# Moving the operands of a depthwise convolution from SBUF into the free columns of their PSUM banks

## What is computed

```python
def causal_depthwise_conv(u, w, b):   # y[t] = sum_k w[k] * u[t - 2 + k] + b, three taps
    ...

h = rms_norm(x, g_pre_ffn[i])
u = causal_depthwise_conv(h @ w_up[i], conv_w[i], conv_b[i])     # 1024 -> 2 * 2816
gate, val = jnp.split(u, 2, axis=-1)
f = (jax.nn.gelu(gate, approximate=True) * val) @ w_down[i]      # 2816 -> 1024
x = x + rms_norm(f, g_post_ffn[i])
...
km = rms_norm_2(km.reshape(b, -1, MEM_HEADS, MEM_HEAD_DIM), mem_qk_norm[1])   # second layer, 4 heads of 128
```

## Time and profile before

| | before |
|---|---|
| median of 3 executions | 882.14 us (881.25 to 884.82) |
| profiled execution | 886.73 us, of which span 885.0 us |
| PE busy | 832.1 us (94%) |
| DVE busy | 660.9 us (75%) |
| ACT busy | 499.7 us (56%) |
| POOL busy | 321.6 us (36%) |
| mean granted TensorE clock | 0.988 |
| L1930, the taps | 66.9 us |
| chain that ended last | PE 57%, DVE 23%, ACT 9%, issue 7%; DVE YC L1930 5% |

### The profile page before, as it was taken

How to read it: one execution, slowest core, us unless ns; L and a number is a source line. 1 busy time by engine, 2 the same in 40 slices (tenths; PEclk the granted TensorE clock), 3 DMA queues, 4 the chain that set the end, 5 groups by cost and what they waited for, 6 DMA issues and landing times.

```text
span 885.0 us, 16964 instructions
## 1 busy us (share of the span) xinstructions
PE 832.1 (94%) x6722; PEld 794.3 (90%) x6722; DVE 660.9 (75%) x981; ACT 499.7 (56%) x914; POOL 321.6 (36%) x148
## 2 busy tenths in 40 slices
PE   4999999999899999998999889988999999999998
PEld 3998889899899999797999779877998899999998
DVE  6695863898889997657899988865756576667774
ACT  6665645844555666866765574457555545444441
POOL 3743222112332333443656453422454233323321
PEclk8999999999999999999999998999999999999999
DMA  5743234344564756461756452322445457666651
GB/s 206 267 161 98 76 91 141 117 144 158 168 213 149 222 160 190 142 190 49 247 168 201 152 171 73 96 96 72 137 153 168 163 152 224 196 190 192 185 173 49
DMA packets 57246, 137.18 MB, mean 155 GB/s; under 512 B 6352, under 2 KB 27088, under 8 KB 57168
## 3 DMA queue, kind: packets, MB, share of 16 engines
q1 hardware_dynamic: 57168, 136.11, 48.4%
HBM read 135.03 MB, written 1.05 MB: 154 GB/s over the span
## 4 chain that ended last, share of the span: by engine, by line
PE 57%; DVE 23%; ACT 9%; issue 7%; DMA 2%; POOL 1%; SPq 0%; DVEq 0%; ACTq 0%
PE PROD L619 11%; PE PROD L620 10%; PE PROD L621 10%; DVE wlo L1622 6%; DVE YC L1930 5%; ACT whi L1109 4%; DVE RS L1630 3%; PE PROD L681 3%; PE OP L821 2%; DMA raw<-stream 2%; PE OP L619 2%; PE TP L621 2%; PE TP L620 2%; PE TP L619 2%; PE OP L621 2%
## 5 line engine op out<-in xcount | busy, mean ns | idle before, releaser
L602 POOL TENSOR_TENSOR wlo<-raw,whi 128x1024 fp32r<-128x1024 f32 x124 | 318.2, 2572 | 542.8 <-ACT whi L1109 518.6
L619 PE MATMUL PROD<-HA,whi 128*128 128x256 f32 x1080 | 306.8, 284 | 14.4 <-DVE HA L1651 6.0
L620 PE MATMUL PROD<-HA,wlo 128*128 128x256 f32 x1080 | 301.8, 279 | 0.0
L621 PE MATMUL PROD<-HA,whi 128*128 128x256 f32 x1080 | 301.7, 279 | 0.0
L1109 ACT ACTIVATE whi<-raw 128x1024 fp32r<-128x1024 f32 x252 | 261.8, 1053 | 39.7 <-PE PROD L621 21.1
L1622 DVE TENSOR_TENSOR wlo<-raw,whi 128x1024 fp32r<-128x1024 f32 x128 | 192.7, 1510 | 77.8 <-ACT whi L1109 77.7
L619 PEld LDWEIGHTS PROD<-HA,whi 128*128 128x128 f32 x1080 | 205.8, 191 | 17.7 <-DVE HA L1651 6.4
L620 PEld LDWEIGHTS PROD<-HA,wlo 128*128 128x128 f32 x1080 | 205.5, 190 | 0.6 <-issue 0.5
L621 PEld LDWEIGHTS PROD<-HA,whi 128*128 128x128 f32 x1080 | 205.1, 190 | 0.0
L1930 DVE SCALAR_TENSOR_TENSOR YC<-Y,CV,YC 128x255 f32<-128x255 f32 x88 | 66.9, 762 | 2.2 <-ACT YC L1333 0.7
L619 PE MATMUL OP<-HA,whi 128*128 128x256 f32 x200 | 57.2, 286 | 1.5 <-DVE wlo L1622 0.8
(11 more groups left out here) (322 smaller groups left out, 1648.4 us busy)
## 6 DMA issues: line engine op xcount, KB each, us to landing
raw<-stream SPq DMA_DIRECT2D x197, 512.0 KB, 4.0
raw<-stream SPq DMA_DIRECT2D x144, 128.0 KB, 2.4
raw<-stream SPq DMA_DIRECT2D x28, 256.0 KB, 2.9
raw<-stream SPq DMA_DIRECT2D x4, 384.0 KB, 3.4
X<-xT SPq DMA_DIRECT2D x2, 512.0 KB, 5.6
out<-X SPq DMA_DIRECT2D x8, 128.0 KB, 2.0
KMEM<-memT SPq DMA_DIRECT2D x1, 512.0 KB, 5.4
VMEM<-memT SPq DMA_DIRECT2D x1, 512.0 KB, 6.1
```

Of the source, the lines that this page charges most:

```text
L602: nc.gpsimd.tensor_tensor(wlo[:, n % NSPLIT, :], raw[:, n % NRAW, :], whi[:, n % NSPLIT, :].bitcast(F32), ALU.subtract).then_inc(lo_pool, 1)
L619: nc.tensor.matmul(dst, wh, hi, start=start, stop=False, skip_group_check=True)
L620: nc.tensor.matmul(dst, wl, hi, start=False, stop=False, skip_group_check=True)
L621: last = nc.tensor.matmul(dst, wh, lo, start=False, stop=stop, skip_group_check=True)
```

## The change

The gate half's scaled product is written into columns 256 to 511 of its own bank and read there by ScalarE and by the taps, whose sum stays in `YC` in SBUF. The up half's scaled product stays in `UU` in SBUF, while its sum of taps, the product with the gelu and the sources of the high and the low part lie in columns 256 to 511 of its bank. So every instruction of VectorE on these halves has one tensor input in SBUF and one in PSUM; the low part (`act_low`) becomes a tensor_tensor. A gate bank is freed by its second tap, no longer by the scaling, and an up bank by the low part of its chunk. The memory statistics leave the rotation for the two banks of `TP`, and the first down pass waits until both their roots are taken. TensorE's matmuls, the stream's tiles, the transfers and the order of work on each engine stay as they were.

```diff
--- before.py
+++ after.py
@@ -204,12 +204,14 @@
 
 
 PLAIN_STATS = ("gk", "gv", "kcT", "vc", "lnmean")
-FFN_OUTS = {(n, m) for n in ("up", "up2") for m in range(2 * FC)} | {("stat", "memk0"), ("stat", "memk1")}
+FFN_OUTS = {(n, m) for n in ("up", "up2") for m in range(2 * FC)}
 BANK, PREV, FREE_COUNT = {}, {}, {}
 _last, _seen, _c = {}, [-NBANK + i for i in range(NBANK)] + [0], [0] * 8
 for _i, _o in enumerate(OUTS):
     if _o[0] in ("down", "down2"):
         _k = 4 + _o[1] // 2
+    elif _o in (("stat", "memk0"), ("stat", "memk1")):
+        _k, PREV[_o] = 6 + int(_o[1][-1]), None
     elif _o[0] == "wo":
         _k = _o[1] // 2
         _seen[_k] = _i
@@ -221,7 +223,7 @@
         PREV[_o] = _last.get(_k)
         _last[_k] = _o
     BANK[_o] = _k
-    if _o[0] != "brnsa" and (_o[0] != "stat" or _o[1] in PLAIN_STATS):
+    if _o[0] != "brnsa" and (_o[0] != "up" or _o[1] % 2 == 0) and (_o[0] != "stat" or _o[1] in PLAIN_STATS):
         _c[_k] += 1
         FREE_COUNT[_o] = _c[_k]
 
@@ -429,7 +431,7 @@
         conv0 = sem("conv0")
         gelu_done = sem("gelu_done")
         act_out = sem("act_out")
-        conv_done = sem("conv_done")
+        up_ready = sem("up_ready")
         gate_tanh = sem("gate_tanh")
         gated = sem("gated")
         act2_out = sem("act2_out")
@@ -465,8 +467,13 @@
             if k <= NBANK:
                 bank = PROD[:, k, :] if k < NBANK else OP[:, :]
                 return bank[:, o[1] % 2 * S:o[1] % 2 * S + S] if o[0] == "wo" else bank
+            if o[0] == "stat":
+                return TP[:, (k - 6) * 512:(k - 5) * 512]
             at = (k - 4) % 2 * 512 + o[1] % 2 * S
             return (SC if k < 6 else TP)[:, at:at + S]
+
+        def scaled_half(o):
+            return PROD[:, BANK[o], S:2 * S] if BANK[o] < NBANK else OP[:, S:2 * S]
 
         def wait_product(eng, o):
             last = last_block(o)
@@ -482,6 +489,8 @@
 
             if o[0] == "brnsa":
                 eng.wait_ge(a_lo, SP0["y"] + o[1] + 1)
+            elif o[0] == "up" and o[1] % 2:
+                eng.wait_ge(a_lo, SP0["a"] + o[1] // 2 + 1)
             elif o in FREE_COUNT:
                 eng.wait_ge(y_free[BANK[o]], FREE_COUNT[o])
             else:
@@ -927,6 +936,8 @@
                                 stat(f"memk{i}", KSQ[:, 2 * S * i:2 * S * (i + 1)], wide=True)
                     if q in DOWN_AFTER:
                         c0 = 2 * DOWN_AFTER[q]
+                        if up == "up":
+                            pe.wait_ge(rt_ready, RT["memk1"] + 1)
                         pe.wait_ge(a_lo, need_a + c0 + 2)
                         for m in range(8):
                             partial(m, c0), partial(m, c0 + 1)
@@ -1326,24 +1337,29 @@
 
                 o = ("up", 2 * j + g)
                 ahead(o)
-                wait_freed(act, o)
+                act.wait_ge(up_ready, 2 * j + g + 1)
+                if g == 0 and j >= 2:
+                    act.wait_ge(gelu_done, j - 1)
+                ch = g * FC + j
+                src, dst = UU[:, j % 2, 1, :], scaled_half(o)
+                if g == 0:
+                    src, dst = dst, YC[:, j % 2, 0, :]
+                nc.scalar.activation(dst, src, ACT.Identity,
+                                     scale=CV[:, COL["conv_w"] + 2 * 2 * FC + ch:COL["conv_w"] + 2 * 2 * FC + ch + 1],
+                                     bias=CV[:, COL["conv_b"] + ch:COL["conv_b"] + ch + 1]).then_inc(conv0, 1)
+
+            def gelu(j):
+
+                wait_freed(act, ("up", 2 * j))
                 if j >= 2:
                     act.wait_ge(act_out, j - 1)
-                ch = g * FC + j
-                nc.scalar.activation(YC[:, j % 2, g, :], UU[:, j % 2, g, :], ACT.Identity,
-                                     scale=CV[:, COL["conv_w"] + 2 * 2 * FC + ch:COL["conv_w"] + 2 * 2 * FC + ch + 1],
-                                     bias=CV[:, COL["conv_b"] + ch:COL["conv_b"] + ch + 1]).then_inc(conv0, 1)
-
-            def gelu(j):
-
-                act.wait_ge(conv_done, 2 * j + 1)
                 nc.scalar.activation(G1[:, j % 2, 0, :], YC[:, j % 2, 0, :],
                                      ACT.Gelu_apprx_tanh).then_inc(gelu_done, 1)
 
             def act_high(j):
 
                 act.wait_ge(act_out, j + 1)
-                high(ACTS, j, G1[:, j % 2, 1, :])
+                high(ACTS, j, scaled_half(("up", 2 * j + 1)))
 
             for j in range(FC):
                 flushed = j % 2 == 0 and j // 2 - 1 in DOWN_AFTER
@@ -1916,23 +1932,27 @@
             def up_scaled(j, g):
                 o = ("up", 2 * j + g)
                 wait_product(dve, o)
-                nc.vector.tensor_tensor(UU[:, j % 2, g, :], product(o)[:, 0:S], RSF[:, :], ALU.mult).then_inc(
-                    free(o), 1)
+                dst = scaled_half(o) if g == 0 else UU[:, j % 2, 1, :]
+                nc.vector.tensor_tensor(dst, product(o)[:, 0:S], RSF[:, :], ALU.mult).then_inc(up_ready, 1)
 
             def conv_rest(j, g):
 
-                y, src = YC[:, j % 2, g, :], UU[:, j % 2, g, :]
+                o = ("up", 2 * j + g)
+                y, src = YC[:, j % 2, 0, :], scaled_half(o)
+                if g:
+                    y, src = src, UU[:, j % 2, 1, :]
                 dve.wait_ge(conv0, 2 * j + g + 1)
-                wait_freed(dve, ("up", 2 * j + g))
+                dve.wait_ge(up_ready, 2 * j + g + 1)
                 for tap in (1, 0):
                     shift = 2 - tap
                     at = COL["conv_w"] + tap * 2 * FC + g * FC + j
                     ins = nc.vector.scalar_tensor_tensor(out=y[:, shift:S], in0=src[:, 0:S - shift],
                                                          scalar=CV[:, at:at + 1], in1=y[:, shift:S], op0=ALU.mult,
                                                          op1=ALU.add)
-                    if tap:
+                    if tap or g:
                         link(ins)
-                ins.then_inc(conv_done, 1)
+                if g == 0:
+                    ins.then_inc(free(o), 1)
 
             def down_tiles(o):
 
@@ -1943,11 +1963,16 @@
             def act_mul(j):
 
                 dve.wait_ge(gelu_done, j + 1)
-                dve.wait_ge(conv_done, 2 * j + 2)
-                if j >= 2:
-                    dve.wait_ge(a_lo, SP0["a"] + j - 1)
-                nc.vector.tensor_tensor(G1[:, j % 2, 1, :], G1[:, j % 2, 0, :], YC[:, j % 2, 1, :],
-                                        ALU.mult).then_inc(act_out, 1)
+                bank = scaled_half(("up", 2 * j + 1))
+                nc.vector.tensor_tensor(bank, bank, G1[:, j % 2, 0, :], ALU.mult).then_inc(act_out, 1)
+
+            def act_low(j):
+
+                o = ("up", 2 * j + 1)
+                dve.wait_ge(a_hi, SP0["a"] + j + 1)
+                dve.wait_ge(act_out, j + 1)
+                nc.vector.tensor_tensor(ACTS[:, j, S:2 * S], scaled_half(o), ACTS[:, j, 0:S].bitcast(F32),
+                                        ALU.subtract).then_inc(a_lo, 1)
 
             for j in range(FC):
                 flushed = j % 2 == 0 and j // 2 - 1 in DOWN_AFTER
@@ -1958,13 +1983,13 @@
                 ahead(("up", 2 * j))
                 up_scaled(j, 1)
                 if j and not flushed:
-                    low(ACTS, "a", j - 1, G1[:, (j - 1) % 2, 1, :])
+                    act_low(j - 1)
                 conv_rest(j, 0)
                 ahead(("up", 2 * j + 1))
                 if j % 2 and j // 2 in DOWN_AFTER:
                     conv_rest(j, 1)
                     act_mul(j)
-                    low(ACTS, "a", j, G1[:, j % 2, 1, :])
+                    act_low(j)
                     down_tiles(("up", 2 * j + 1))
                 if j in MEMK_AT:
                     i = MEMK_AT[j]
```

More of the change, by code:

```diff
@@ L1328, in conv_first @@
                 ahead(o)
-                wait_freed(act, o)
-                if j >= 2:
-                    act.wait_ge(act_out, j - 1)
+                act.wait_ge(up_ready, 2 * j + g + 1)
+                if g == 0 and j >= 2:
+                    act.wait_ge(gelu_done, j - 1)
                 ch = g * FC + j
-                nc.scalar.activation(YC[:, j % 2, g, :], UU[:, j % 2, g, :], ACT.Identity,
+                src, dst = UU[:, j % 2, 1, :], scaled_half(o)
+                if g == 0:
+                    src, dst = dst, YC[:, j % 2, 0, :]
+                nc.scalar.activation(dst, src, ACT.Identity,
                                      scale=CV[:, COL["conv_w"] + 2 * 2 * FC + ch:COL["conv_w"] + 2 * 2 * FC + ch + 1],
@@ L1337, in gelu @@
             def gelu(j):
-                act.wait_ge(conv_done, 2 * j + 1)
+                wait_freed(act, ("up", 2 * j))
+                if j >= 2:
+                    act.wait_ge(act_out, j - 1)
                 nc.scalar.activation(G1[:, j % 2, 0, :], YC[:, j % 2, 0, :],
```

## The result

| | before | after |
|---|---|---|
| median in the comparison | 883.2 us (880.4 to 886.24, 10 executions) | 874.34 us (869.04 to 880.55, 10 executions) |
| profiled execution | 886.73 us, span 885.0 | 875.89 us, span 874.2 |
| PE / DVE / ACT / POOL busy | 832.1 / 660.9 / 499.7 / 321.6 us | 827.0 / 638.9 / 499.1 / 314.9 us |
| chain that ended last | PE 57%, DVE 23%, ACT 9%, issue 7% | PE 76%, DVE 12%, ACT 6%, issue 4% |
| mean granted TensorE clock | 0.988 | 0.988 |

The changed kernel is 1.0% faster: the ratio is 0.9900, with an interval of 0.9868 to 0.9932. The forecast was 873.0 us.

The account below looks back on a forecast made before the run. TensorE's first FFN was taken to lose 10.7 us to stops that late VectorE work causes and to a slow pace. Less 0.6 for one stop and 1.0 for the median, 882.1 - 9.1 = 873.0 us; range 871 to 876, chance 0.66.

Parts of the forecast that it names:

- The stretches: First FFN's taps on VectorE: 24.6 us of stretches beside GpSimd's subtractions go, plus 1.0 for a low part.
- Rival A: VectorE's tiles meet the subtractions instead, half of each stretch returns: 5.1 us saved, 877.0 us; chance 0.12.
- The price of PSUM: VectorE in the first FFN: 0 to 11 ns for each of 154 instructions, at most 1.7 us, hidden under TensorE.
- ScalarE: Its convolutions writing PSUM: bounded by 0.1 us either way, none taken, since ScalarE waits for the products anyway.
- The stops: TensorE's six stops in the first FFN, 7.9 us with restarts, go, but for 0.6 us left near output 25.
- slow pace: First FFN's matmuls on TensorE: 0.0044 us more for each of some 135 + 331, 2.1 us in all.
- Rival B: The slow pace is drawn anew; through the whole first FFN it keeps back 6.6 us: 878.0 us; chance 0.10.
- The median: Undisturbed runs may stop less in this FFN than the profiled one: 1.0 us taken off the gain, leaving 9.1.
- Rival D: Banks held longer while stretches stay: output 39 waits for a low part, 3.6 + 1.7 us slower, 887.4; chance 0.07.

Follow-up runs that it names:

- e3_gate: The changed kernel with the up half back in SBUF and only the gate half in PSUM, longer hold of banks kept: 880.92 us, ratio 0.9964 to the kernel before.
- e4_up: The changed kernel with the gate half back in SBUF and only the up half in PSUM, longer hold kept: 882.70 us, ratio 0.9998 to the kernel before.
- e5_allvec: The kernel before with all 66 weight tiles of the first FFN on VectorE, none on GpSimd, data in SBUF: 878.57 us, ratio 0.9913.
- e9_look: The changed kernel unaltered, profiled once more to see the pace of its matmuls: 871.14 us.
- e2_hold: The changed kernel with all its waits and longer hold of banks, but both halves' data back in SBUF: 885.54 us, ratio 1.0022 to the kernel before.
- e1_stats: The kernel before with only the memory statistics moved to TP and the first down pass's wait: 882.96 us, ratio 0.9991.

## Why the prediction was right

- **The stretches.** 24.6 us were to leave the taps; their sum fell from 66.9 to 42.3 us. VectorE's busy time in the whole kernel fell by 22.0 us in the profiled pair, for the 24 foretold. That a PSUM operand keeps a tap clear of GpSimd had been read from 42 taps of the later layer, and e3_gate and e4_up show it half by half. Rival A, a tile meeting the subtraction instead, didn't come: five tiles stretched before, five after.
- **The price of PSUM.** It lies at the low end of 0 to 11 ns for most: taps +2 ns at the most in the median, the product 433 for 426, the gate's scaling 432 for 418, three ns over my bound; the low part got 8 ns cheaper (416 for 424), as another instruction: a tensor_tensor for a scalar_tensor_tensor. The 65 ns for each that the Trainium skill gives ("VectorE: DVE Perf Modes", section on the TRN2 errata), 8.5 us in all as an estimate, are not there.
- **ScalarE.** I bounded its write to PSUM by 0.1 us either way: it takes 556 ns where writing SBUF took 602, and the high part 384 for 417. The two sorts of convolution together save 44 x 0.045 = 2.0 us of ScalarE's own time. The stops go without that saving too, as e5_allvec shows.
- **The stops.** All went, the tail's too. The low part of chunk 10 ended at 254.26, 1.0 us sooner than worked out, and output 25 started at 255.28 without a wait: 1.0 us of slack for the 0.3 foretold. So the 0.6 us left for a stop there was the one term too many, and the FFN gave 10.6 us for the 10.1 forecast. Timelines of DVE and PE, after:

```profile
253.84 0.42 DVE L1974 TENSOR_TENSOR ACTS<-PROD,ACTS 128x256 fp32r<-128x256 f32 x1
```

```profile
255.28 0.28 PE L628 MATMUL PROD<-HA,whi 128*128 128x256 f32 x1
```

- **GpSimd's part.** The longest stop of TensorE before, 2.28 us ahead of the pass behind group 3, was ended by GpSimd's low part, and the prediction didn't say how VectorE's relief would end it. The timelines of the kernel before show the chain. ScalarE waits for VectorE's product (`act_mul`) until 219.87, makes its high part and only then the copies, the first of which GpSimd waits for:

```profile
219.87 0.42 ACT L1132 ACTIVATE ACTS<-G 128x256 fp32r<-128x256 f32 x1 [2.15 <-DVE G L1949]
220.19 2.94 ACT L1109 ACTIVATE whi<-raw 128x1024 fp32r<-128x1024 f32 x3
...
221.32 2.35 POOL L602 TENSOR_TENSOR wlo<-raw,whi 128x1024 fp32r<-128x1024 f32 x1 [13.11 <-ACT whi L1109]
```

  In the kernel after the same product is made earlier, ScalarE's high part starts at 213.98, and GpSimd's subtraction at 215.39, 5.9 us sooner.

- **Order of the sum.** By the table the stops of the kernel before (6.62 us and 7 x 0.25) make 8.4 us and its slow pace 2.1, of the 10.6; the prediction had 7.9 and 2.1. Both went. The second was luck as far as it was argued: I had only said that the start of the long stretch isn't moved, and e5_allvec, where no stop is left either, ran slow. Nor is a stop needed for a change of pace, as I had it: in e9_look it changed across the statistics. Rival B is real, and its 6.6 us were rightly priced (6.8 measured); only it did not strike in a profile of the changed kernel. Its 878.0 leaves out the 1.6 us that the forecast takes off: 873.0 + 6.6 = 879.6 is what the forecast's own sum gives, near the four slower executions at 877.6 to 880.6.
- **The median.** The 1.0 us taken off gave 9.1; the comparison's medians differ by 883.2 - 874.34 = 8.9. That hits, but the reason given for it isn't shown: the profiled pair differs by 10.8.
- **Rival D** was misplaced. I had it decide at output 39 and cost 5.4 - 1.8 = 3.6 us; e2_hold puts it at output 24, 4.6 us, by the gate's taps, and at output 13, 2.2 us, and the ratio makes it 0.0022 x 884.6 = 1.9 us slower (-0.6 to +4.5) for the 3.6 and 1.7 that I had added up. I had walked through the up halves' slack alone and overlooked that a gate's bank is now freed behind two taps, either of which may be a stretched one. Nothing hung on it, since the stretches did go.

## What to carry to other kernels

Where an engine is late, look first whether the same instruction has two durations and what runs beside the long ones: here 13 of 88 taps carried 24.6 us, all beside GpSimd's subtractions, and either one operand in PSUM or GpSimd's work elsewhere ended it. Free columns of a product's own bank are a home for that operand, but the bank's release decides: count the outputs until the bank comes round again, since one step later brought six stops, 6.9 us, and with the slow pace beside them the whole gain was gone. And relief of an engine is worth what the bounding engine waits for it: some 24 us off VectorE took 8.4 us of stops from the first FFN and nothing from the second, which had none.

## What the runs showed of the hardware

- **Two paces of TensorE at one clock.** Matmuls of 256 columns with their weight loads start 0.1133 or 0.1177 us apart, both at a granted clock of 1.00 (2.4 GHz): 1326 or 1276 in 150 us. The slow pace held through 1548 matmuls without a stop, the quick one through 1561, and it changed only at a break: a stop, or the four matmuls of 512 columns of the memory statistics.
- **The clock behind a stop.** Behind the 4.6 us stop of e2_hold the granted clock fell for about 4 us. Busy time by stretch, e2_hold:

```profile
250.00:260.00 10.00, 6.68 (x59) 6.49 (x58) 7.94 (x11) 5.33 (x7) 3.84 (x2) 1.00 0.51 149
261.00:265.00 4.00, 3.70 (x20) 3.70 (x21) 3.93 (x9) 3.65 (x6) 0.00 (x0) 0.62 0.67 217
265.00:275.00 10.00, 9.87 (x84) 9.67 (x84) 9.64 (x16) 5.84 (x10) 2.63 (x1) 0.98 0.56 166
```

  A mean of 0.62 between the levels of 1.0 and 0.5 (2.4 and 1.2 GHz) means some three quarters of the stretch at the lower one; TensorE is busy for 3.70 us of it and makes 20 matmuls, where 33 would go. e4_up shows 0.59 for 4 us behind its stop of 3.6 us, and e1_stats 0.66 for 5 us behind one of 3.0 us; in the kernel before, whose longest was 2.3 us, the clock stayed at 1.00. By the table these three kernels' long stops cost 1.6 to 1.8 us more than idle time and restart.
- **ScalarE and PSUM.** An activation of 128x256 with scale and bias takes 556 ns when it writes PSUM, and 546 to 564 when it reads it, against 602 with both in SBUF, 38 to 56 ns less. (With both in SBUF it takes 588 and 589 in the two runs without GpSimd in this FFN.) The Trainium skill ("VectorE: DVE Perf Modes", section on the TRN2 errata) has 224 fixed cycles for ScalarE from SBUF and 172 from PSUM, at 1.2 GHz 43 ns (an estimate): for reading PSUM this difference agrees with the runs, where the difference in its row for VectorE doesn't.
